# Modulation products from split weights in a fused two-block transformer kernel, spread one unit at a time between the other units

## What is computed

```python
silu_c = jax.nn.silu(c)[:, None, :]
silu_cc = jax.nn.silu(c_ctx)[None, None, :]
for i in range(DEPTH):
    sh1, sc1, gt1, sh2, sc2, gt2 = jnp.split(silu_c @ ada_w[i] + ada_b[i], 6, axis=-1)
    csh1, csc1, cgt1, csh2, csc2, cgt2 = jnp.split(silu_cc @ ada_w[i] + ada_b[i], 6, axis=-1)
    h = rmsnorm(x, norm1_g[i]) * (1.0 + sc1) + sh1
    ...
    x = x + gt1 * y
    x = x + gt2 * sq_relu_mlp(rmsnorm(x, norm2_g[i]) * (1.0 + sc2) + sh2, mlp_w1[i], mlp_w2[i])
```

## Time and profile before

| | us |
|---|---|
| median of 3 runs | 4295.11 |
| the runs | 4288.22 to 4296.49 |
| the profiled execution | 4307.66 |
| its span, first to last instruction | 4305.9 |

### The profile page before, as it was taken

How to read it: one execution, slowest core, us unless ns; L and a number is a source line. 1 busy time by engine, 2 the same in 40 slices (tenths; PEclk the granted TensorE clock), 3 DMA queues, 4 the chain that set the end, 5 groups by cost and what they waited for, 6 DMA issues and landing times.

```text
span 4305.9 us, 59574 instructions
## 1 busy us (share of the span) xinstructions
PE 3780.9 (88%) x24624; PEld 2900.2 (67%) x24624; DVE 2115.9 (49%) x3456; ACT 1501.9 (35%) x2684; POOL 161.4 (4%) x408
## 2 busy tenths in 40 slices
PE   7888889999995877788768999896999999679999
PEld 4644466777883556778627888575788777457886
DVE  3355544333447573566354445635444554535445
ACT  4333434122224472233243333333333342434333
POOL 0000000000000010333110000000000000000000
PEclk9989999999996998899879999795999999789999
DMA  4011112232111554566412222110123222012221
GB/s 178 31 64 53 40 39 88 108 127 108 59 59 51 153 150 153 143 158 162 117 70 77 99 97 107 40 71 25 69 88 107 90 76 88 1 44 88 99 97 59
DMA packets 295293, 380.57 MB, mean 88 GB/s; under 512 B 240496, under 2 KB 243440, under 8 KB 260336
## 3 DMA queue, kind: packets, MB, share of 16 engines
q1 hardware_dynamic: 281648, 330.88, 23.9%
q10 hardware_dynamic: 13376, 45.87, 2.9%
HBM read 331.61 MB, written 45.11 MB: 87 GB/s over the span
## 4 chain that ended last, share of the span: by engine, by line
PE 73%; DVE 11%; ACT 7%; DMA 3%; issue 2%; POOL 2%; SPq 1%; ACTq 0%; DVEq 0%; POOLq 0%
PE ps L253 17%; PE ps L254 17%; PE ps L255 17%; PE ps L327 4%; PE ps L720 2%; PE ps L701 2%; PE ps L1188 1%; PE ps L1190 1%; PE ps L1189 1%; DMA s_it<-rt 1%; DVE mx L1441 1%; DVE nsm L793 1%; ACT s L3192 1%; DVE xml L1446 1%; PE ps L3156 1%
## 5 line engine op out<-in xcount | busy, mean ns | idle before, releaser
L238 ACT ACTIVATE whi<-panel 128x1024 fp32r<-128x1024 f32 (+1 forms) x524 | 442.2, 844 | 667.0 <-PE ps L255 631.3
L245 DVE TENSOR_TENSOR wlo<-panel,whi 128x1024 fp32r<-128x1024 f32 (+1 forms) x524 | 503.8, 963 | 331.5 <-ACT whi L238 322.2
L253 PE MATMUL ps<-xh,whi 128*128 128x512 f32 x1184 | 481.2, 406 | 43.4 <-DVE xl L2359 23.0
L253 PE MATMUL ps<-dh,whi 128*128 128x512 f32 (+1 forms) x1280 | 474.9, 371 | 0.0
L254 PE MATMUL ps<-dh,wlo 128*128 128x512 f32 (+1 forms) x1280 | 472.7, 369 | 0.0
L255 PE MATMUL ps<-dl,whi 128*128 128x512 f32 (+1 forms) x1280 | 470.9, 368 | 0.0
L254 PE MATMUL ps<-xh,wlo 128*128 128x512 f32 x1184 | 466.4, 394 | 0.0
L255 PE MATMUL ps<-xl,whi 128*128 128x512 f32 x1184 | 465.3, 393 | 0.0
L253 PE MATMUL ps<-hh,whi 128*128 128x512 f32 (+1 forms) x960 | 351.6, 366 | 26.7 <-DVE hl L447 26.7
L254 PE MATMUL ps<-hh,wlo 128*128 128x512 f32 (+1 forms) x960 | 339.3, 353 | 0.0
L255 PE MATMUL ps<-hl,whi 128*128 128x512 f32 (+1 forms) x960 | 338.8, 353 | 0.0
(11 more groups left out here) (448 smaller groups left out, 5964.5 us busy)
## 6 DMA issues: line engine op xcount, KB each, us to landing
panel<-in_w SPq DMA_DIRECT2D x248, 1024.0 KB, 4.8
ld<-s_fe ACTq DMA_DIRECT2D x16, 1024.0 KB, 6.9
s_fe<-x SPq DMA_DIRECT2D x37, 256.0 KB, 2.8
ld<-s_fe ACTq DMA_DIRECT2D x24, 256.0 KB, 4.6
ld<-s_fe ACTq DMA_DIRECT2D x8, 768.0 KB, 6.9
vv<-s_fe ACTq DMA_DIRECT2D x24, 256.0 KB, 7.0
s_fe<-x SPq DMA_DIRECT2D x40, 128.0 KB, 2.3
s_ys<-yy SPq DMA_DIRECT2D x16, 256.0 KB, 3.2
```

The lines of the kernel that those rows point to most:

```text
L238: e.activation(unit(u)[0][:, 0:kc, :], w, ACT.Copy).then_inc(*w_hi.up(u))
L245: e.tensor_tensor(lo[:, 0:kc, :], w, hi[:, 0:kc, :].bitcast(F32), SUB).then_inc(*w_lo.up(u))
L253: e.matmul(out, hi[:, k, :], xh, start=k == 0, stop=False)
```

## The change

The modulation weights go the way of all other weights. Their panels are split into 96 units of 8 blocks (128 outputs each), every unit through `act_hi` and `dve_lo`. The conditionings are split too, once: `SCS` holds four stationary columns (high parts of the two vectors, then low parts). One single-pass product a block takes high and low weights together as 256 moving columns, so 8 products a unit give a 4 x 256 result; it holds the sums of all four combinations. Two tiny products with `SEL` (4 x 2) turn it and add up high and low. One order of all units (`_order`) replaces the order of panels: 16 modulation units in `ada0`, 17 in `att` (two buffers there), 7 in `wo`, 56 in `mlp0`, in the last two stages each between two other units. The hook is gone; a modulation unit is a tile of kind "a" in the list of `Mlp`, and `Proj` takes them likewise.

```diff
+    def mixed(main, more, first):
+        out = []
+        for i, x in enumerate(main):
+            out += [x] + more[i - first:i - first + 1 if i >= first else 0]
+        return out
...
+    out = ada(0, "ada0", 0, 16) + many("q", 4, "qkv") + many("k", 1, "qkv") + many("v", 1, "qkv")
+    out += ada(0, "att", 16, 33) + ada(0, "wo", 33, 34) + mixed(many("wo", 4, "wo"), ada(0, "wo", 34, 40), 0)
+    out += mixed(mlp("m1", "m2", 0, "mlp0"), ada(0, "mlp0", 40, 48) + ada(1, "mlp0", 0, 48), 1)
...
     def ada_mm(e, n):
...
-        if n > 8:
-            e.wait_ge(*ad_dv.at(n - 1))
-        elif n > 1:
-            e.wait_ge(*ad_dv.at(n - 2))
+        w2 = unit(ADAU[n])
+        e.wait_ge(*w_lo.at(ADAU[n]))
+        if n > 3:
+            e.wait_ge(*ad_dv.at(n - 4 if n < 16 else 13 if n == 16 else n - 1))
         for k in range(8):
-            i = e.matmul(row, SC[:, k, :], w[:, k * 256:k * 256 + 256], start=k == 0, stop=k == 7)
+            i = e.matmul(ada_bank(n)[0:4, 0:256].rearrange("p (a b) -> p a b", a=2), SCS[:, k, :], w2[:, :, k, :],
+                         start=k == 0, stop=k == 7)
...
     def ada_tr(e, n):
...
-        e.transpose(out[:, 0:2], AROW[n % 2][:, 0:P], ID[0:2, 0:2])
-        e.transpose(out[:, 2:4], AROW[n % 2][:, P:2 * P], ID[0:2, 0:2]).then_inc(*ad_tr.up(n))
+        e.matmul(out, AROW[n % 2][:, 0:P], SEL[:, :], start=True, stop=False)
+        e.matmul(out, AROW[n % 2][:, P:2 * P], SEL[:, :], start=False, stop=True).then_inc(*ad_tr.up(n))
...
     def att_dve(e):
...
         for n in range(NAU + 2):
-            if 0 < n < 17:
-                ada_add(e, 7 + n)
+            if 0 < n < 18:
+                ada_add(e, 15 + n)
+            if 0 < n < 16:
+                dve_lo(e, ADAU[17 + n])
...
     class Proj:
...
         def pe(self, e):
             for m in range(8):
+                if self.ada:
+                    if m > 0:
+                        ada_tr(e, self.ada + m - 1)
+                    if m < 7:
+                        ada_mm(e, self.ada + m)
...
         def dve(self, e):
             for m in range(8):
+                if self.ada and m < 7:
+                    dve_lo(e, ADAU[self.ada + m] + 2)
+                if self.ada and m > 0:
+                    ada_add(e, self.ada + m - 1)
...
     class Mlp:
...
+            self.next = {t: x[4] + 2 for t, x in enumerate(order) if x[3] == 0 and t > 1 and x[4] + 2 <= u}
...
         def pe(self, e):
+            for t, (kind, q, m, s, u, f, j) in enumerate(self.tiles):
+                if kind == "a":
+                    if q > self.a0:
+                        ada_tr(e, q - 1)
+                    ada_mm(e, q)
+                    continue
...
         def act(self, e):
                 if t in self.next:
                     act_hi(e, self.next[t])
+                if kind == "a":
+                    ada_row(e, q)
...
         def dve(self, e):
+                if t in self.next:
+                    dve_lo(e, self.next[t])
+                if kind == "a" and q > self.a0:
+                    ada_add(e, q - 1)
```

More of the change, by code:

```diff
@@ L90, with _order, panel, ada @@
 MLP_STEPS = [("f", 0)] + [s for q in range(8) for s in ([("f", q + 1)] if q < 7 else []) + [("s", q)]]
[L93 to L99, removed]
+def _order():
+    def panel(key, stage, kc=8):
+        return [(key, stage, kc, m) for m in range(16 // kc if kc else 1)]
+    def ada(layer, stage, a, b):
+        return [(("ada", layer, i // 2), stage, 8, i % 2) for i in range(a, b)]
+    def mixed(main, more, first):
[3 more added lines that the diff above has]
+        return out
     def mlp(a, b, layer, stage):
@@ L103, in mlp @@
         for kind, q in MLP_STEPS:
-            seq += [((a if kind == "f" else b, layer, 2 * q + j), stage, 8 if kind == "f" else 4) for j in range(2)]
-        return seq
[L107 to L121, removed]
+            for j in range(2):
+                seq += panel((a if kind == "f" else b, layer, 2 * q + j), stage, 8 if kind == "f" else 4)
+        return seq
+    def many(name, n, stage):
+        return [x for j in range(n) for x in panel((name, j), stage)]
@@ L122, in _panels @@
+    for a in ("qa", "ka", "va", "hq", "hf", "hi", "hg", "evo"):
+        out += many(a, 4 if a == "evo" else 2, "even")
     for l in range(2):
         if l == 1:
-            out += [((a, j), "odd", 8) for a in ("oq", "ok", "ov", "odo") for j in range(4)]
+            for a in ("oq", "ok", "ov", "odo"):
+                out += many(a, 4, "odd")
         out += mlp("f1", "f2", l, f"ffn{l}")
-        out += [(("pg", l, j), f"ple{l}", 8) for j in range(4)]
+        out += [x for j in range(4) for x in panel(("pg", l, j), f"ple{l}")]
@@ L127, in _panels @@
+    return out
+def _panels():
+    out = []
+    for key, stage, kc, _ in _order():
+        if key not in [x[0] for x in out]:
+            out.append((key, stage, kc))
     return out + [(("pp", l), f"ple{l}", 0) for l in range(2)]
@@ L138, in _units @@
     started = {}
-    for p, (_, stage, kc) in enumerate(PANELS):
+    for key, stage, kc, m in _order():
         if kc == 0:
@@ L142, in _units @@
         first = started.setdefault(stage, len(out))
[L143 to L149, removed]
+        b = (len(out) - first) % (2 if stage in ("att", "feat", "odd") else 3)
+        of_panel.setdefault(PIDX[key], []).append(len(out))
+        out.append((PIDX[key], kc, m, b, held.get(b), stage))
+        held[b] = len(out) - 1
     return out, of_panel, started
 UNITS, PUNITS, FIRST = _units()
+ADAU = [PUNITS[PIDX["ada", n // 48, n % 48 // 2]][n % 2] for n in range(96)]
 def program(nc, ins, out_d, scratch):
@@ L227, in unit, with unit_free @@
     def unit(u):
-        b, stage = UNITS[u][3], PANELS[UNITS[u][0]][1]
-        return SPLIT[stage][b]
+        return SPLIT[UNITS[u][5]][UNITS[u][3]]
+    def unit_free(u):
+        s = ad_mm if PANELS[UNITS[u][0]][0][0] == "ada" else unit_done[UNITS[u][5]]
+        return s.at("unit", u)
     def act_hi(e, u):
@@ L350, in ada_add @@
+        if part in (1, 4) and i == 7:
             which = 0 if part == 1 else 1
@@ L846, in program, with __init__ @@
     class Proj:
-        def __init__(self, u0, mm, ac, dv, src, segs, add, tail, then):
-            self.u0, self.mm, self.ac, self.dv, self.src, self.segs, self.add = u0, mm, ac, dv, src, segs, add
-            self.tail, self.then = tail, then
+        def __init__(self, name, mm, ac, dv, src, segs, add, tail, then, ada=None):
+            self.units = [u for j in range(4) for u in PUNITS[PIDX[name, j]]]
+            self.mm, self.ac, self.dv, self.src, self.segs, self.add = mm, ac, dv, src, segs, add
+            self.tail, self.then, self.ada = tail, then, ada
         def key(self, m, s):
-            return ("unit", self.u0 + m) if s == len(self.segs) - 1 else ("tile", m, s)
+            return ("unit", self.units[m]) if s == len(self.segs) - 1 else ("tile", m, s)
         def pe(self, e):
@@ L869, in act @@
             for m in range(9):
-                if m < 6:
-                    act_hi(e, self.u0 + m + 2)
+                if self.ada and m < 7:
+                    act_hi(e, ADAU[self.ada + m] + 2)
+                if not self.ada and m < 6:
+                    act_hi(e, self.units[m] + 2)
                 if m == 7:
@@ L877, in act @@
                         self.tail.tile_act(e, t, self.dv.at("res", t))
+                if self.ada and m < 7:
+                    ada_row(e, self.ada + m)
+                    if m < 6:
+                        act_hi(e, self.units[m] + 2)
         def dve(self, e):
```

240 lines of the change are left out of this document (127 added, 113 removed).

## The result

| | before | after |
|---|---|---|
| median, us | 4295.8 (4288.22 to 4300.77, 4 runs) | 4585.71 (4582.47 to 4589.32, 4 runs) |
| the profiled execution, us | 4307.66 | 4589.32 |

The ratio is 1.0677, interval 1.0658 to 1.0695: slower, as forecast, and 54 us beyond the forecast of 4532, inside the range. On the scale of the profiled execution the sum said 4544.8, and it is 4589.3; some 44 us are missing from the sum.

The account below looks back on a forecast made before the run. TensorE, busy 88% of the span, was taken as the bound. 138.8 + 23.8 - 1 - 13 - 3 + 91.5 = +237.1 gave 4544.8 on the profiled execution's scale, 4532 us on the runs' scale, range 4405 to 4620.

Parts of the forecast that it names:

- mlp0 without the clock: mlp0: waits and new products cost 238.8 us against 100 us of panel products that go, +138.8 us.
- clock in mlp0: mlp0: 55 new waits lower the granted clock, 1.5 us lost for each.
- wo with its clock: wo: seven units of 0.96 and six waits of 2.84, +23.8; one split off the norm's chain, -1; clock 1.5 a wait.
- att: att: VectorE's next turn starts about 1.0 us earlier in 16 steps, less 3 for two splits: -13 us, between -41 and +8.
- ada0: ada0: 16 units at 1.5 to 2.2 us each end between 43 and 54; -3 us, between -8 and +5.
- qkv and rest: Stages without modulation units: no term in the sum; the part behind mlp0's last modulation unit was to stay unchanged.
- The wait: mlp0, wo: product q waits for the bias add of q-1, behind high and low part; 2.84 us lost, 61 waits.
- The pace of the product: Modulation product, four stationary columns: 0.96 us a unit taken; rival: f32 pace, 3.6 us a unit, 4760 us, chance 0.04.
- The turn: mlp0: 0.3 us a unit taken beside the 0.96 product, so without waits mlp0 would be 29 us shorter.
- the rival of 4231: Rival: no wait comes; mlp0 -29, wo +9, att as much as -41, ada0 -3, 4231 us; chance 0.05.
- The clock: mlp0 and wo: 61 new waits at 1.5 us each, +91.5 us; rival that it stays up, 4440, chance 0.12.
- the upper end of 2.6: Clock loss per wait if all of att's shortfall counts, 39.6 / 15; by the skill's rule some 159 us in all.

Follow-up runs that it names:

- the filling: Three idle f32 products of 512 columns behind each att modulation product, against the kernel with the moved turn: 4324.81 us, ratio 1.0067.
- c_fill_acc: The kernel with the moved turn plus 16 products of 128 columns a unit, a single turn product and the filling in att: 4313.49 us, ratio 1.0038.
- the kernel with the moved turn: Changed kernel with turn and bias add of q moved between the two tiles of the next main unit: 4340.17 us, ratio 1.009.

## Why the prediction was right, and where its sum was off

| part, us | predicted | measured |
|---|---|---|
| mlp0 without the clock | +138.8 | +138 (775.3 - 637.3) |
| clock in mlp0 | +82.5 | +71 |
| wo with its clock (23.8 - 1 + 9) | +31.8 | +37.2 |
| att | -13 | +12.3 |
| ada0 | -3 | +12.7 |
| qkv and rest | 0 | +10.1 |
| sum | +237.1 | +281.5 |

**The wait** is the mechanism as predicted, with its count, its releaser and its length: 2.57 us from the unit's end to the product where 2.68 was forecast, 3.75 behind "f" where it was 3.99. What decided it, that the high part of the next modulation unit needs the buffer of the unit that just ended, is the 3.27 us for which ScalarE stands until 846.44, released by TensorE. That mlp0 without the clock comes out at 138 is in part luck. The waits are 33 x 0.11 + 22 x 0.24 = 9 us less and the products 56 x 0.04 = 2 less; the slower pace of all products by the shift brings 3 back (629.9 against 626.9 with and without it); about 7 more were not traced.

**The pace of the product** was the open price. With four stationary columns it is 0.92 a unit, next to the 0.96 that was taken and far from 3.6. That the wait is not run past holds too.

**The turn** was mis-sized: `mlp0` without waits was to be 29 us shorter, and it is 1.0 shorter (636.3). In that place it costs 0.73 at full clock where 0.3 was taken, 56 x 0.43 = 24 us; the shift adds 3. In the forecast this did not show, because behind a unit the turn lies inside the wait. It shows in the rival of 4231: with the wait taken away the kernel is at 4340, slower than before and not 65 us faster. That rival's condition was tested and its price was wrong by 109 us: above all the gain of att (-41 taken, +4.5 found), then the turn (24), the shift (16) and ada0 (-3 taken, +9.3 found).

**The clock** costs 1.29 a wait in mlp0 where 1.5 was taken from att's shortfall. In wo the six waits with their clock cost 114.6 - 85.1 = 29.5, 4.9 each, where 2.84 + 1.5 = 4.3 was in the sum; how wait and clock share this was not measured there. The product at 799.96 takes 1.87, but the one at 848.97 has 1.08, and records of 0.63 begin only at 850.13. All 22 products behind an "f" unit, after pauses of 3.75 us, take 1.65 to 1.87; of the 33 behind an "s" unit, after about 2.6 us, 25 take 1.07 to 1.10 and 8 take 1.18 to 1.49. The Trainium skill (TensorE: Matmul & The Clock Gate, "HAM oscillation") describes a kernel in which every burst after a pause starts slow, with pauses that are longer beside their bursts than these. Here that holds behind the "f" units and for the most part not behind the "s" units, so the cost lies well under the upper end of 2.6, near which the prediction put it by this rule.

**att** is the term with the wrong sign; +12.3 lies outside its own bounds of -41 to +8, and the other kernels with the same att give +2.8 and more. Its step was that with 2.6 us less product VectorE's next turn starts earlier. This left out that the f32 product had kept TensorE busy: with 1 us in its place the clock of att fell from 0.88 to 0.75, and the scores (those of 256 columns, 394 to 491 ns) and transposes (325 to 389) on the chain got longer. The prediction applied the clock to the new waits alone and not to the work taken out. With the filling these are back at 392 and 303 ns, and 15 us of the total with them. But the clock isn't all of it: halving the turn, which in att stands ahead of a step's scores, shortened the stage about as much with the clock left low (366.9 us at 0.79), and the two together gave no more in the profiles. How the loss divides between clock and turn stays open. The gain of 13 isn't found with the filling (370.0 against 372.2), though single profiles differ here: the shifted kernel before has 365.3.

**ada0** was to end its modulations at 43 to 54 us and does so at 64.1. The start at 13 was right (12.65). The 1.5 to 2.2 us a unit were not right: TensorE at the lower rate takes 2.74 from one product to the next, 1.80 for the product and 0.94 for the turn, and this is more than ScalarE's and VectorE's 1.5.

**The stages without a change** were set to zero by saying nothing of them. The shift of 136 bytes costs 16 us in the kernel before and 16 in c_fill_acc (4313.49 against 4297.83). This term was missing altogether.

## What to carry to other kernels

When a buffer ring of n is walked by two kinds of work in turn, look at whose release the preparation of the next needs, and keep small results that a waiting product needs ahead of long preparations on the same engine's program. Work taken from TensorE in a stage that already has pauses need not make the stage shorter, since what is left can run at the lower clock; price it with the clock of that stage. And compare the pace of untouched stages first: a changed address can cost as much as the edit gives.

## What the runs showed of the hardware

- Idle products on TensorE raised the granted clock (0.86 to 0.99 in mlp0, 0.76 to 0.91 in att). They shortened mlp0 by 56 us although its waits were left as they were, and att by 6.7 us; with the shorter turn att was the same with and without them.
- A shift of SBUF addresses by 136 bytes slows 512-column single-pass products from 0.2274 to 0.2289 us from start to start, with nothing else changed. Which address matters and why stays open.
- A granted clock of 1.00 at the start of a trace can mean that nothing was recorded. In the changed kernel it reads 1.00 from 12 to 48 us, where 8 products take 1.87 us, but the first record of the clock in that trace lies at 61.6 us. In the kernel with the moved turn the records begin at 16.2 us, and the same stretch reads 0.70. The distance between starts decides.

```profile
12.00:48.00 36.00, 31.39 (x138) 19.81 (x138) 20.37 (x30) 21.42 (x37) 0.00 (x0) 1.00 0.69 268
```

- Full f32 products with 4 stationary rows of 128 and 2 columns moving have a price however little they compute: set into a stream, one costs 0.40 us and two cost 0.63, and the product behind them 0.10 more. That is about four fifths of the 0.92 that the unit's own product takes.
